# Differential attention in a two-layer hybrid block: both maps' scores as pairs of 64-row products, three passes per unit in place of four, and two row transposes in place of four

## What is computed

```python
q = q.reshape(b, s, DIFF_HEADS, 2, DIFF_HEAD_DIM)      # 4 heads, 2 maps, 64 wide
k = k.reshape(b, s, DIFF_HEADS, 2, DIFF_HEAD_DIM)
q1, q2 = rope(q[..., 0, :]), rope(q[..., 1, :])
k1, k2 = rope(k[..., 0, :]), rope(k[..., 1, :])
def block(q_start, q1b, q2b):                          # 128 queries at a time
    a1 = masked_softmax(einsum(q1b, k1) * 64 ** -0.5)
    a2 = masked_softmax(einsum(q2b, k2) * 64 ** -0.5)
    return einsum(a1 - lam * a2, v)                    # v is 128 wide
```

## Time and profile before

| | |
|---|---|
| median of 3 runs | 2683.39 us |
| the 3 runs | 2674.73, 2683.39, 2686.8 us |
| span of the profiled execution | 2675.5 us |
| mean granted TensorE clock | 0.986 |
| PE busy (PEld busy) | 2538.8 us, 95% (2177.0 us, 81%) |
| DVE, ACT, POOL busy | 57%, 41%, 38% |
| transfers | 242.68 MB, 91 GB/s |

### The profile page before, as it was taken

How to read it: one execution, slowest core, us unless ns; L and a number is a source line. 1 busy time by engine, 2 the same in 40 slices (tenths; PEclk the granted TensorE clock), 3 DMA queues, 4 the chain that set the end, 5 groups by cost and what they waited for, 6 DMA issues and landing times. The chain is left out here.

```text
span 2675.5 us, 43064 instructions
## 1 busy us (share of the span) xinstructions
PE 2538.8 (95%) x13054; PEld 2177.0 (81%) x13054; DVE 1533.2 (57%) x3045; ACT 1094.8 (41%) x2503; POOL 1013.6 (38%) x1161
## 2 busy tenths in 40 slices
PE   6999989999899999999989999999998999999997
PEld 5999967878688888888889998777786888888886
DVE  4666555482655454577656665454727445445885
ACT  4444554272522232344444445433624322223444
POOL 2455432173254545201044555221823444441012
PEclk9999999999999999999989999999999999999999
DMA  5111011023233233573331101011222333236633
GB/s 180 29 34 36 19 37 38 12 81 142 71 110 101 91 110 109 183 257 99 99 110 32 35 19 41 5 38 59 89 102 63 114 107 113 82 110 240 210 97 122
DMA packets 238651, 242.68 MB, mean 91 GB/s; under 512 B 27904, under 2 KB 171008, under 8 KB 238464
## 3 DMA queue, kind: packets, MB, share of 16 engines
q1 hardware_dynamic: 238464, 240.43, 27.8%
HBM read 172.75 MB, written 67.63 MB: 90 GB/s over the span
## 5 line engine op out<-in xcount | busy, mean ns | idle before, releaser
L2414 POOL TENSOR_TENSOR fw_a_lo<-fw_a_raw,fw_a_hi 128x512 fp32r<-128x512 f32 x132 | 179.5, 1360 | 467.9 <-DVE fw_s_raw L1997 467.9
L2414 POOL TENSOR_TENSOR fw_s_lo<-fw_s_raw,fw_s_hi 128x512 fp32r<-128x512 f32 x176 | 229.3, 1315 | 52.0 <-ACT fw_s_hi L1487 52.0
L723 PE MATMUL banks<-ht_hi,da_hi 128*128 128x512 f32 x496 | 192.9, 389 | 0.0
L723 PE MATMUL banks<-ht_lo,da_hi 128*128 128x512 f32 x496 | 192.9, 389 | 0.0
L723 PE MATMUL banks<-ht_hi,da_lo 128*128 128x512 f32 x496 | 192.9, 389 | 0.0
L723 PE MATMUL banks<-w_diff_hi,ht_hi 128*128 128x384 f32 x512 | 179.7, 351 | 6.4 <-DVE ht_lo L1674 4.4
L723 PE MATMUL banks<-w_diff_hi,ht_lo 128*128 128x384 f32 x512 | 171.9, 336 | 0.0
L723 PE MATMUL banks<-w_diff_lo,ht_hi 128*128 128x384 f32 x512 | 171.5, 335 | 0.0
L2242 POOL TENSOR_TENSOR qk_rot<-rope_a,rope_b 128x512 f32<-128x512 f32 x64 | 82.6, 1291 | 207.1 <-DVE rope_b L1703 207.1
L1731 DVE TENSOR_REDUCE stats<-banks 128x1 f32<-128x1024 f32 (+3 forms) x192 | 138.3, 748 | 32.3 <-PE banks L924 27.4
L723 PE MATMUL banks<-h_t_hi,fw_s_hi 128*128 128x512 f32 x352 | 139.9, 398 | 13.2 <-DVE h_t_lo L2001 8.2
(11 more groups left out here) (357 smaller groups left out, 7474.9 us busy)
## 6 DMA issues: line engine op xcount, KB each, us to landing
da_raw<-act_scratch SPq DMA_DIRECT2D x154, 256.0 KB, 2.6
fw_a_raw<-in_w_gate_dram SPq DMA_DIRECT2D x88, 256.0 KB, 3.1
act_scratch<-act_s SPq DMA_DIRECT2D x66, 256.0 KB, 2.9
w_diff_raw<-in_w_in_dram SPq DMA_DIRECT2D x24, 512.0 KB, 5.8
fw_a<-in_w_up_dram SPq DMA_DIRECT2D x44, 256.0 KB, 3.2
fw_a_raw<-in_w_up_dram SPq DMA_DIRECT2D x44, 256.0 KB, 2.9
act_scratch<-act_zero SPq DMA_DIRECT2D x44, 256.0 KB, 2.4
act_scratch<-act_one SPq DMA_DIRECT2D x44, 256.0 KB, 2.8
```

What stands on the lines that cost most here:

```text
L723: mm = pe.matmul(bank, lhsT, rhs, start=first and i == 0, stop=last and i == len(pairs) - 1, skip_group_check=resumes)
L2414: pool.tensor_tensor(w[1][:], w[2][:], w[0][:].bitcast(F32), ALU.subtract).then_inc(S["f_lo"], 1)
```

## The change

`dk` is split in two tiles of 128 rows, `dk_hi` and `dk_lo`, in which rows 0 to 63 belong to map 0 and rows 64 to 127 to map 1, and `dq_hi` and `dq_lo` are laid out in the same way. `qk_rot` holds each map once: 256 columns, written by POOL in one addition of half the width, transposed by PE in two transposes in place of four. ACT's two copies and DVE's two operations for hi and lo then have 128 rows by 128 columns each.

`diff_scores` issues hi*hi, hi*lo and lo*hi (the term lo*lo is gone) as products over 64 rows, the two maps in turn. For a chunk of keys that is six products of 64 rows in place of four of 128. Both masks come at the end, one after the other. The wait on `s_exp` stands once, ahead of both maps, at 2a: for the exponentials of both maps of the unit before.

The diff:

```diff
--- before.py
+++ after.py
@@ -238,9 +238,8 @@
     X = sb("X", [P, T, D], F32, XREG)
     mixed_rows = sb("mixed_rows", [P, T, D], F32, XREG)
 
-    dq_hi = sb("dq_hi", [P, 2, SEQ], F32R, XREG)
-    dq_lo = sb("dq_lo", [P, 2, SEQ], F32R, XREG + 8 * KB)
-    dk = sb("dk", [P, 2, SEQ], F32R, XREG + 16 * KB)
+    dq_hi, dq_lo, dk_hi, dk_lo = (sb(name, [P, SEQ], F32R, XREG + 4 * KB * i)
+                                  for i, name in enumerate(("dq_hi", "dq_lo", "dk_hi", "dk_lo")))
 
     dv = [sb(f"dv{i}", [P, 2, P], F32R, XREG + (24 + i) * KB if i < T else MREG + (18 + i - T) * KB) for i in range(V_SLOTS)]
 
@@ -262,7 +261,7 @@
 
     rope_a = [sb(f"rope_a{i}", [P, 4, 2, 32], F32, MREG + (8 + i) * KB) for i in range(2)]
     rope_b = [sb(f"rope_b{i}", [P, 4, 2, 32], F32, MREG + (10 + i) * KB) for i in range(2)]
-    qk_rot = [sb(f"qk_rot{i}", [P, 4, 2, 64], F32, MREG + (12 + 2 * i) * KB) for i in range(2)]
+    qk_rot = [sb(f"qk_rot{i}", [P, 4, 64], F32, MREG + (12 + 2 * i) * KB) for i in range(2)]
     d_mx = [sb(f"d_mx{i}", [P, P], F32, MREG + 22 * KB + 512 * i) for i in range(2)]
     d_sum = [sb(f"d_sum{i}", [P, P], F32, MREG + 20 * KB + 512 * i) for i in range(2)]
     m_sum = [sb(f"m_sum{i}", [P, MLA_V], F32, slots[1] + 8 * KB + 256 * i) for i in range(2)]
@@ -788,9 +787,9 @@
                 def diff_transpose(u):
                     pe.wait_ge(S["rope_sum"], L * PER["rope_sum"] + u + 1)
                     bank = take_ring()
-                    for v in range(4):
-
-                        tr = pe.transpose(bank[:, tokens(v)], qk_rot[u % 2][:, v].rearrange("p c d -> p (c d)"), ident[:])
+                    for v in range(2):
+
+                        tr = pe.transpose(bank[:, tokens(v)], qk_rot[u % 2][:, 2 * v:2 * v + 2].rearrange("p m d -> p (m d)"), ident[:])
                     tr.then_inc(S["tr_done"], 1)
                     assert qk_ring[u] == ring[0]
 
@@ -798,18 +797,21 @@
                     t = tile_of(a)
                     if a % T == 0:
                         pe.wait_ge(S["tr_free"], L * PER["tr_free"] + qk_ring[a + T - 1])
+                    if a >= 1:
+                        pe.wait_ge(S["s_exp"], L * PER["s_exp"] + 2 * a)
+                    qt = tokens(t)
+                    for c in range(0, (t + 1) * P, 512):
+                        n = min(512, (t + 1) * P - c)
+                        diagonal = c + n == (t + 1) * P
+                        keys = slice(c, c + n)
+                        for part, (q, k) in enumerate(((dq_hi, dk_hi), (dq_hi, dk_lo), (dq_lo, dk_hi))):
+                            for m in range(2):
+
+                                rows_m = slice(64 * m, 64 * m + 64)
+                                pe.matmul(SCORE[m][:, keys], q[rows_m, qt], k[rows_m, keys], start=part == 0,
+                                          stop=part == 2 and not diagonal)
                     for m in range(2):
-                        j = 2 * a + m
-                        if j >= 2:
-                            pe.wait_ge(S["s_exp"], L * PER["s_exp"] + j - 1)
-                        for c in range(0, (t + 1) * P, 512):
-                            n = min(512, (t + 1) * P - c)
-                            diagonal = c + n == (t + 1) * P
-                            keys = dk[:, m, c:c + n]
-                            mm = products(SCORE[m][:, c:c + n], [(dq_hi[:, m, tokens(t)], keys), (dq_lo[:, m, tokens(t)], keys)],
-                                          last=not diagonal)
-                        mm = pe.matmul(SCORE[m][:, tokens(t)], ident_r[:], mask_r[:], start=False, stop=True)
-                        mm.then_inc(S["s_done"], 1)
+                        pe.matmul(SCORE[m][:, qt], ident_r[:], mask_r[:], start=False, stop=True).then_inc(S["s_done"], 1)
 
                 def weighted(bank, hi, lo, v, width):
 
@@ -1279,9 +1281,9 @@
                 def diff_qk(u):
                     t = tile_of(u)
                     r = round_ring()
-                    bank = banks[:, TR_BANKS[r % 2], :].rearrange("p (a m n) -> p a m n", a=2, m=2)
-                    act.activation(dq_hi[:, :, tokens(t)], bank[:, 0], ACT.Copy, scale=DIFF_SCALE)
-                    act.activation(dk[:, :, tokens(t)], bank[:, 1], ACT.Copy).then_inc(S["tr_hi"], 1)
+                    bank = banks[:, TR_BANKS[r % 2], :]
+                    act.activation(dq_hi[:, tokens(t)], bank[:, 0:P], ACT.Copy, scale=DIFF_SCALE)
+                    act.activation(dk_hi[:, tokens(t)], bank[:, P:2 * P], ACT.Copy).then_inc(S["tr_hi"], 1)
 
                 def exponentials(j, dst, a, m, t):
                     act.wait_ge(S["s_max"], L * PER["s_max"] + j + 1)
@@ -1720,11 +1722,11 @@
                 def diff_low(u):
                     t = tile_of(u)
                     r = low_ring()
-                    bank = banks[:, TR_BANKS[r % 2], :].rearrange("p (a m n) -> p a m n", a=2, m=2)
-                    dve.scalar_tensor_tensor(dq_lo[:, :, tokens(t)], bank[:, 0], DIFF_SCALE, dq_hi[:, :, tokens(t)].bitcast(F32),
+                    bank = banks[:, TR_BANKS[r % 2], :]
+                    dve.scalar_tensor_tensor(dq_lo[:, tokens(t)], bank[:, 0:P], DIFF_SCALE, dq_hi[:, tokens(t)].bitcast(F32),
                                              ALU.mult, ALU.subtract)
-                    low = dk[64:P, :, tokens(t)]
-                    dve.tensor_tensor(low, bank[64:P, 1], low.bitcast(F32), ALU.subtract).then_inc(S["tr_free"], 1)
+                    dve.tensor_tensor(dk_lo[:, tokens(t)], bank[:, P:2 * P], dk_hi[:, tokens(t)].bitcast(F32), ALU.subtract)\
+                        .then_inc(S["tr_free"], 1)
 
                 def negated_max(j, a, m, t):
                     dve.wait_ge(S["s_done"], L * PER["s_done"] + j + 1)
@@ -2235,19 +2237,15 @@
                 inverse_roots(0, [(4, T), (0, 4)], 0)
                 weights(0)
 
-                def rotation(n, a, b, dst, copies):
-
-                    pool.wait_ge(S["rope_ab"], L * PER["rope_ab"] + n + 1)
-                    a, b = (x[:].rearrange("p v s d -> p v (s d)").unsqueeze(2).to_broadcast([P, 4, copies, 64]) for x in (a, b))
-                    return pool.tensor_tensor(dst[:] if copies > 1 else dst[:].unsqueeze(2), a, b, ALU.add)
-
                 def diff_rotation(u):
                     if not 0 <= u < DIFF_UNITS:
                         return
                     if u >= 2:
 
                         pool.wait_ge(S["tr_done"], L * PER["tr_done"] + qk_ring[u - 2])
-                    rotation(u, rope_a[u % 2], rope_b[u % 2], qk_rot[u % 2], 2).then_inc(S["rope_sum"], 1)
+                    pool.wait_ge(S["rope_ab"], L * PER["rope_ab"] + u + 1)
+                    pool.tensor_tensor(qk_rot[u % 2][:], *(x[u % 2][:].rearrange("p v s d -> p v (s d)") for x in (rope_a, rope_b)),
+                                       ALU.add).then_inc(S["rope_sum"], 1)
 
                 def diff_root(a):
                     if not 0 <= a < DIFF_UNITS:
```

## The result

| | before | after |
|---|---|---|
| median | 2680.61 us (4 runs, 2674.73 to 2686.8) | 2701.43 us (4 runs, 2700.43 to 2702.26) |
| ratio to before | 1 | 1.0074 [1.0061, 1.0088] |
| span of the profiled execution | 2675.5 us | 2700.5 us |
| mean granted TensorE clock | 0.986 | 0.977 |

The change makes the kernel 0.74% slower, 20.8 us on the medians. The forecast was 2697.7 us, in a range of 2677 to 2718. Every run on record takes 1.8 us more than its own span (2702.26 us for 2700.5), so the profiled execution of before lies 3.3 us under its median, and that of after 0.8 us over its own. All that follows is taken from the spans' rows, so it has to add up to 25.0.

What follows compares the result with a forecast made beforehand. PE, busy 95% of the span, was taken to bound the kernel by its own instruction order. +6.8 us without the clock and +7.5 for clock falls made +14.3: span 2689.8, plus 7.9 gives median 2697.7 us, range 2677 to 2718.

Steps and rivals of the forecast that it cites:

- PE's order of instructions is the time: Differential attention: shortening PE's chain counts in full; work taken from DVE, ACT and POOL counts nothing unless PE waits.
- Streaming saved, pairs side by side: Scores: two maps' products run together, saving one pass a unit, from 0.46 us at t = 7 to 0.11 at t = 0.
- Switching: Scores, between 128 and 64 rows: 0.44 us a unit, less 0.12 for dropped late starts, net 0.32.
- The first two units: Each head's start: waiting for both maps' exponentials adds 1.90 us, t = 6 saves 0.38, together +1.52 us a head.
- Transposes: Two fewer save 0.18 us a unit in seven units, -1.26 a head; in the last unit the gain becomes wait.
- Sum without the clock: Differential attention: score, head-start and transpose terms together +0.85 us a head, +6.8 over 8 heads.
- The clock at head starts: The longer pause of 3.6 us makes TensorE's clock fall at about seven of eight starts, five more: +7.5 us.
- the offset from span to median: Whole kernel: the median of the runs shown stood 7.9 us above the profiled span, added to the forecast span.
- Rival 2: Scores: pairs don't run side by side at 512 columns, or only in part; full case +50 us, 2747; chance 0.06.
- Rival 3: Unit exits: short drain behind long products, only 0.10 a unit lost; 2676. Faster by over 0.5%: chance 0.07.
- Rival 1: Saving covers the waits, by few clock falls or switches at 0.15: close to no change; 0.37 with Rival 3's mild part.

Runs made afterwards that it cites:

- e_same_rows: Changed kernel with map 1's scores computed from map 0's rows, so both products of a pair need the same array rows: 2768.96 us (one run).
- e_mid_mask: Changed kernel with both masks of the diagonal chunk put before its last pair of score products instead of after it: 2729.65 us, ratio 1.0178.
- e_fill: Changed kernel with 13 unused products of 512 columns put into PE's pause at each head start: 2680.81 us, ratio 0.9998.
- e_four_tr: Changed kernel with each of its two transposes issued twice, four per unit again: 2709.34 us, ratio 1.0106.
- b_fill: Kernel before with five unused products of 512 columns put into its short pause at each head start: 2681.48 us, ratio 0.9991.
- b_shift8: Kernel before with 8 unused products of 512 columns ahead of each layer's first projection: 2686.25 us (one run).
- e_proj_first: Changed kernel with half a projection (12 products) moved ahead of the scores of each head's second unit, into the pause: 2669.0 us, ratio 0.9955.
- b_proj_first: Kernel before with half a projection (12 products) moved ahead of the scores of each head's second unit: 2670.74 us, ratio 0.9958.
- a_best: e_proj_first with four unused products of 512 columns added ahead of the wait for `s_exp`: 2668.93 us, ratio 0.9951.

## Why the prediction was right

**PE's order of instructions is the time.** Right. The wait for both maps' exponentials cost nothing outside the head starts: PE waits for them eight times in the whole trace. POOL's part is down by 12.3 us a layer in the touched stage and ACT's by 6.4, and none of that shows in the time.

**Streaming saved, pairs side by side.** Right: 0.23 us a pair at 512 columns with one start, 0.46 when both use the same rows (e_same_rows).

**Switching.** The net of 0.32 a unit holds, its pieces don't. Entering costs 0.09 more than usual (0.15 was taken). The step from the last pair to the mask costs 0.10 more (0.33 for 0.23; 0.18 was taken). The two masks cost 0.27 for 0.12, 0.15 more (0.11 taken). And the late second product (0.34 for the first distance, 0.11 too long, as 0.29 before, 0.06 too long in each map) does not vanish, as the prediction had it, but is paid once. That is 0.09 + 0.10 + 0.15 + 0.11 - 0.12 = 0.33 net, so the errors of the pieces cancel, which is luck. The blocks came out as worked out: 0.84 for 0.87 at t = 0, 1.61 for 1.61 at t = 5. e_mid_mask measured an excursion by itself, 0.29 for 0.44.

**The first two units.** Head start +1.93 us (5.60 - 3.76 and 0.09 at the entry) for +1.90, the pause 3.57 for 3.56. Only the distance from the mask to the maximum was mis-sized by more than 0.05 us, 0.36 for 0.25. The block of t = 6 can be read in e_fill, where the clock is at 1.00: 273.82 to 275.52 by the next two rows of its timeline, 1.70 us for 1.72:

```profile
275.25 0.44 PE L818 MATMUL banks<-mask_r,ident_r 128*128 128x128 f32 x2
275.52 0.41 PE L722 MATMUL banks<-w_mla_hi,ht_hi 128*128 128x416 f32 x1
```

**Transposes.** Mis-sized: 0.22 saved a unit for 0.18 (e_four_tr). In the last unit of a head the gain did become wait: PE waits 4.4 us for `dv` over the whole trace, for 3.0 before and 3.0 in e_four_tr.

**Sum without the clock.** Forecast +6.8. e_fill has no fall in the touched stages: 274.1 us against 270.0 (b_fill), less the 1.9 gained ahead of it, is +2.2 a layer, 4.4 in all. The larger part of the difference, 0.04 x 56 = 2.2 us, is the transposes.

**The clock at head starts.** Right in kind: 8 falls of 8 at 1.5 us (seven were forecast), six more than before, so 9 us for 7.5. Together with the 4.4 that makes 13.4, which the windows give as 13.3, beside the forecast of 14.3.

**What it missed.** The prediction costed all the rest of the kernel at nothing, without saying so. The rest gave 11.3 us of the 25.0 in the span, by a lower clock in stages whose code is the same. With that the span of after lies 10.7 above the forecast span of 2689.8; the median lies only 3.7 above the forecast, because the offset from span to median, taken as 7.9, was 0.9. The 7.9 is no fixed offset: a run takes 1.8 us more than its own span, and the rest is how far the profiled execution lay under the median. So the forecast is nearer than its sum, and that nearness is luck; measured against its own before, the change cost 20.8 us on the medians for the 14.3 forecast.

**The rivals.** Rival 2 falls (e_same_rows). Rival 3 falls too: behind a long product the way out costs 0.10 and then 0.15 in the masks, and e_mid_mask finds no short drain. Rival 1's price for a switch, 0.15, falls too, and all the clock falls came. But the touched code alone is +13.3 us in the span, just at the 13.4 us that can be told from no change; without the untouched stages' clock the measurement could well have come out as no change. The verdict of slower rests on both.

## What to carry to other kernels

A change that takes a quarter off the streaming of one part can still lose where it lengthens a chain across engines: here both maps now leave PE late, PE pauses 3.6 us in place of 1.5, and the clock falls behind every such pause. Look for the place where two consumers of one resource follow each other without other work between them, and move independent work there; that gave 32 us here, more than the change itself cost, and 11 in the kernel before. And when PE bounds the kernel, compare the untouched stages too, by length and granted clock and in more than one execution, before a difference is put down to an edit.

## What the runs showed of the hardware

- Granted clock and pauses at the head starts: behind a pause of 3.6 us the clock was 0.50 eight times of eight, behind one of 1.5 to 1.7 us two times of eight (before, and two again in b_shift8, not at the same ones), behind one of 1.25 to 1.4 us once of eight (e_proj_first), and with 0.6 us or less left of the pause never (e_fill, b_fill, a_best, b_proj_first). Each fall of 3.4 us cost 1.5 us.
- The same pause of 1.65 us between the same products was followed by a fall in one kernel's execution (after) and by none in another's (before).
- The same products of an untouched stage (1827 or 1828 recorded) took between 351 and 359 us, mostly in step with the granted clock; edits hundreds of microseconds ahead of them and differences between executions are not told apart.
- Two 64-row products on different halves of the rows run fully side by side, and need not alternate in the program: six products as 3 + 3 took the same time as six in turn (2701.41 and 2701.43 us), and started in pairs all the same.
- Leaving 128-row products for 64-row ones and coming back costs 0.29 us (e_mid_mask) to 0.34 us, in three places: 0.09 in front, 0.10 on the way out and 0.15 in the two 128-row products behind.
